# A two-block transformer on one core: first loads in smaller pieces, stacked compression operands, a scaling moved to GpSimd

## The reference, cut to what matters

```python
def first_block(x, ...):
    for l in range(2):
        x = x + 0.5 * swiglu(rms_norm(x, norm_ffn1[l]), w_ffn1_gate[l], w_ffn1_up[l], w_ffn1_down[l])
        x = x + hybrid_mixer(rms_norm(x, norm_mix[l]), w_in[l], ...)
        x = x + 0.5 * swiglu(rms_norm(x, norm_ffn2[l]), ...)
    return rms_norm(x, norm_final)

# inside the first block's mixer
def compress(k, pos, w1, w2):                 # 15 windows of 32 tokens, 2 kv heads: 30 rows
    blocks = k[:, :, cidx, :] + pos
    flat = blocks.reshape(B, G, n_cmp, CMP_LEN * Dh)      # 30 rows of 2048
    return jax.nn.gelu(flat @ w1) @ w2        # w1: 2048 x 256, w2: 256 x 64
kc = compress(k_cmp, pos_ck, w_ck1, w_ck2)
vc = compress(v_cmp, pos_cv, w_cv1, w_cv2)
...
return g[..., 0:1] * o_cmp + g[..., 1:2] * o_slc + g[..., 2:3] * o_win

def second_block(x, ...):                     # two layers: attention, then a SwiGLU FFN
    for l in range(2):
        x = hybrid_layer(...)
    return x                                  # the output
```

## Time and profile before

| | before |
|---|---|
| median of 3 runs | 1820.74 us |
| the profiled execution | 1821.47 us, span 1819.7 us |
| PE busy | 1789.9 us, 98% of the span |
| weight loads of PE busy | 1458.3 us, 80% |
| DVE / ACT / POOL busy | 1124.2 / 929.9 / 206.6 us |
| moved from memory | 173 GB/s over the span |

### The profile page before, as it was taken

How to read it: one execution, slowest core, us unless ns; L and a number is a source line. 1 busy time by engine, 2 the same in 40 slices (tenths; PEclk the granted TensorE clock), 3 DMA queues, 4 the chain that set the end, 5 groups by cost and what they waited for, 6 DMA issues and landing times.

```text
span 1819.7 us, 23649 instructions
## 1 busy us (share of the span) xinstructions
PE 1789.9 (98%) x8740; PEld 1458.3 (80%) x8740; DVE 1124.2 (62%) x1649; ACT 929.9 (51%) x1267; POOL 206.6 (11%) x226
## 2 busy tenths in 40 slices
PE   7999999999999999999999999999999999999999
PEld 6888887788888888877888877778888877788887
DVE  5555687655455555787555479966555589865553
ACT  6444475644444444565544276656444556644441
POOL 0000020000000000300000087200001393100000
PEclk9999999999999999999999999999999999999999
DMA  8556463455555554543554654445555554555551
GB/s 256 185 185 222 137 189 108 139 187 190 213 167 191 184 206 148 183 133 126 185 185 167 229 185 139 161 140 185 185 184 200 160 186 140 185 156 177 187 190 77
DMA packets 221017, 316.21 MB, mean 174 GB/s; under 512 B 14056, under 2 KB 162176, under 8 KB 220672
## 3 DMA queue, kind: packets, MB, share of 16 engines
q1 hardware_dynamic: 220928, 315.03, 53.0%
HBM read 313.94 MB, written 1.05 MB: 173 GB/s over the span
## 4 chain that ended last, share of the span: by engine, by line
PE 88%; DVE 7%; ACT 2%; DVEq 1%; issue 1%; DMA 1%; SPq 0%; ACTq 0%
PE ps L1843 27%; PE ps L1845 26%; PE ps L1844 26%; DVE w_lo L1157 2%; PE ps L1952 2%; PE ps L1853 1%; PE ps L2048 1%; ACT w_hi L679 1%; DVE score L1618 1%; PE ps L2036 1%; PE ps L1987 1%; PE ps L2024 1%; PE ps L2328 1%; DMA raw<-in_w_ffn_up 1%; DVEq L1621 0%
## 5 line engine op out<-in xcount | busy, mean ns | idle before, releaser
L1157 DVE TENSOR_TENSOR w_lo<-raw,w_hi 128x2048 fp32r<-128x2048 f32 (+1 forms) x297 | 675.1, 2297 | 233.0 <-ACT w_hi L679 232.1
L1843 PE MATMUL ps<-w_hi,aT_hi 128*128 128x512 f32 (+2 forms) x1728 | 688.9, 399 | 7.9 <-DVE w_lo L1310 4.8
L1845 PE MATMUL ps<-w_hi,aT_lo 128*128 128x512 f32 (+2 forms) x1728 | 670.4, 388 | 0.0
L1844 PE MATMUL ps<-w_lo,aT_hi 128*128 128x512 f32 (+2 forms) x1728 | 668.6, 387 | 0.0
L679 ACT ACTIVATE w_hi<-raw 128x2048 fp32r<-128x2048 f32 (+1 forms) x297 | 554.5, 1899 | 158.5 <-PE ps L1845 153.8
L1843 PEld LDWEIGHTS ps<-w_hi,aT_hi 128*128 128x128 f32 x1728 | 325.1, 188 | 84.8 <-issue 15.5
L1845 PEld LDWEIGHTS ps<-w_hi,aT_lo 128*128 128x128 f32 x1728 | 324.9, 188 | 68.2
L1844 PEld LDWEIGHTS ps<-w_lo,aT_hi 128*128 128x128 f32 x1728 | 325.7, 188 | 59.3
L729 ACT ACTIVATE att<-ps,rstd 128x256 f32<-128x256 f32 x132 | 55.5, 472 | 377.6 <-PE ps L1845 377.6
L1231 DVE SCALAR_TENSOR_TENSOR att<-ps,rstd,att 128x256 f32<-128x256 f32 x132 | 57.8, 479 | 287.2 <-ACT att L729 287.2
L1843 PE MATMUL ps<-w_hi,gT_hi 128*128 128x512 f32 x528 | 207.1, 392 | 0.0
(11 more groups left out here) (267 smaller groups left out, 1402.4 us busy)
## 6 DMA issues: line engine op xcount, KB each, us to landing
raw<-in_w_in SPq DMA_DIRECT2D x120, 512.0 KB, 4.5
raw<-in_w_ffn_gate SPq DMA_DIRECT2D x88, 512.0 KB, 4.2
raw<-in_w_ffn_up SPq DMA_DIRECT2D x88, 512.0 KB, 5.2
raw<-in_w_ffn_down SPq DMA_DIRECT2D x88, 512.0 KB, 4.4
raw<-in_w_ffn_in SPq DMA_DIRECT2D x88, 512.0 KB, 5.1
raw<-in_w_ffn_out SPq DMA_DIRECT2D x44, 512.0 KB, 4.7
raw<-in_w_out SPq DMA_DIRECT2D x32, 512.0 KB, 4.5
raw<-in_w_ck SPq DMA_DIRECT2D x8, 512.0 KB, 3.9
```

The costliest lines, as they stand in the source:

```text
L1157: V.tensor_tensor(o, a, h, ALU.subtract).then_inc(units_split, 1)
L1843: M(o, ah, wh, start=start, stop=False)
L1844: M(o, ah, wl, start=False, stop=False)
L1845: return M(o, al, wh, start=False, stop=stop)
```

## The change

Four things change.

1. **First loads.** `x` comes in four transfers of 128 rows by 512 columns, units 0 and 1 in halves (two transfers of 256 KB each), interleaved in the order of use; the gains are loaded from ACT's queue. Each quarter of `x` is turned by PE inside the first tile (`first_tile`), and the tile's order is (tokens 0, unit 0), (tokens 1, unit 0), (tokens 0, unit 1), (tokens 1, unit 1) in steps that wait for one quarter and one half unit each. PE does 8 and then 24 transposes of the identity, whose results nobody reads (`busy`). ACT's first table load comes ahead of the first data, and GpSimd makes `ident` before its other constants.
2. **Compression.** High and low parts of the windows lie side by side, 30 + 30 columns (`kflat`, `vflat`), so that one loaded operand holds both; with the high weights and the low weights that is four matmuls a step in place of six (the low-by-low product comes along). The 60 rows are copied out, and a product with `fold` (60x30, two identities on top of each other) turns and adds them; GELU comes after it, on the turned form.
3. **Scaling of the probabilities.** For pairs 0 to 6 of each layer (`SCALED1`) DVE multiplies reciprocal and gate (128x4), and GpSimd scales the probabilities in two TENSOR_TENSORs, 2x128 and 2x256 columns a partition. They stand ahead of `rotate(1304, 8)` in GpSimd's order. PE's `pair_turn(u)` in the compression stands one step later.
4. **The end.** The last 128 tokens are added and stored in two halves of 512 columns.

```diff
+SCALED1 = 7
...
-            def first_unit():
-
-                act.wait_ge(loaded[0], 32)
-                for h, signal in enumerate((half_hi, units_hi)):
-                    nc.scalar.activation(w_hi[:, 0, 1024 * h:1024 * h + 1024], raw[:, 0, 1024 * h:1024 * h + 1024], ACT.Copy)\
-                        .then_inc(signal, 1)
+            def first_half(j, h):
+
+                act.wait_ge(loaded[j] if h else half_loaded[j], 32)
+                part = slice(1024 * h, 1024 * h + 1024)
+                nc.scalar.activation(w_hi[:, j, part], raw[:, j, part], ACT.Copy).then_inc(units_hi if h else half_hi, 1)
...
+                for k in range(SCALED1):
+                    pool.wait_ge(pair_factors, l * SCALED1 + k + 1)
+                    for i, (c, n) in enumerate(((0, P), (P, 2 * P))):
+                        q = pair_p[:, k % 2, :, c:c + n]
+                        o = nc.gpsimd.tensor_tensor(q, q, lanes(pair_factor[:, k % 2, :, i], n), ALU.mult)
+                    o.then_inc(pair_scaled, 1)
                 projected(4)
                 rotate(1304, 8)
...
-                nc.scalar.activation(h1, ps[0:30, 1, :].rearrange("p (k n) -> p k n", k=2), ACT.Gelu_apprx_tanh)\
-                    .then_inc(gelu_done, 1)
+                nc.scalar.activation(h1, ps[0:60, 1, :].rearrange("p (k n) -> p k n", k=2), ACT.Copy)\
+                    .then_inc(h1_copied, 1)
                 exps(5)
                 probs_turned(4)
+                act.wait_ge(h1_T, l + 1)
+                nc.scalar.activation(h1T[:, :, :], ps[:, 6, 384:448].rearrange("p (k n) -> p k n", k=2)[:, :, 0:30],
+                                     ACT.Gelu_apprx_tanh)
+                nc.scalar.activation(vc_h1, ps[:, 6, 448:512].rearrange("p (k n) -> p k n", k=2)[:, :, 0:30],
+                                     ACT.Gelu_apprx_tanh).then_inc(gelu_done, 1)
...
+                        if i == 1 and last:
+                            if n == 0:
+                                dve.wait_ge(last_half, 1)
+                            else:
+                                o.then_inc(x_ready, 1)
+                                dve.wait_ge(units_used, st.used(p_last))
...
+                    if k < SCALED1:
+                        f = pair_factor[:, k % 2, :, :]
+                        assert gates[1] - gates[0] == 12
+                        V.tensor_tensor(f, f, gates1[:, :, gates[0]:gates[0] + 13:12].rearrange("p i e -> p e i"), ALU.mult)\
+                            .then_inc(pair_factors, 1)
+                        return
...
+            def first_turned(n):
+
+                pe.wait_ge(x_loaded[n], 16)
+                turned(x, *FIRST_PARTS[n])
+
+            def first_tile(st):
+
+                for n, (i, j) in enumerate(FIRST_PARTS):
+                    pe.wait_ge(stage_ready, n + 1)
+                    for c in range(4):
+                        if i == 0 and c == 0:
+                            pe.wait_ge(half_split, j + 1)
+                        if i == 0 and c == 2:
+                            split_ready(st, j)
...
+                        if (n, c) == (0, 0):
+                            first_turned(1)
+                        elif (n, c) == (0, 3):
+                            first_turned(2)
+                        elif (n, c) == (1, 3):
+                            first_turned(3)
...
+            def busy(n):
+
+                for _ in range(n):
+                    nc.tensor.transpose(ps[:, 3, 0:P], ident[:, :], ident[:, :])
+
+            pe.wait_ge(ident_ready, 1)
+            busy(8)
             pe.wait_ge(first_gains_loaded, 16)
             nc.tensor.transpose(ps[:, 0, 0:2 * KC], first_rows[:, :], ident[0:2 * KC, 0:2 * KC]).then_inc(gains_T, 1)
+            first_turned(0)
+            busy(24)
...
-                    if c == 2:
+                    if c == 3:
                         pair_turn(u)
...
-                            ah, al = h[:, 30 * k:30 * k + P], lo[:, 30 * k:30 * k + P]
-                            wh, wl = w_hi[:, st.slot(p), w:w + 256], w_lo[:, st.slot(p), w:w + 256]
+                            a = t[:, 60 * k:60 * k + P]
                             o = ps[:, 1, 256 * n:256 * n + 256]
-                            M(o, ah, wh, start=k == 0 and n == 0, stop=False, skip_group_check=True)
-                            M(o, ah, wl, start=False, stop=False, skip_group_check=True)
-                            o = M(o, al, wh, start=False, stop=k == 15, skip_group_check=True)
+                            M(o, a, w_hi[:, st.slot(p), w:w + 256], start=k == 0 and n == 0, stop=False, skip_group_check=True)
+                            o = M(o, a, w_lo[:, st.slot(p), w:w + 256], start=False, stop=k == 15, skip_group_check=True)
```

More of the change, by code:

```diff
@@ L227, in build @@
         rope_loaded = sem("rope_loaded")
-        x_loaded = [sem(f"x_loaded{i}") for i in range(2)]
+        x_loaded = [sem(f"x_loaded{k}") for k in range(4)]
+        half_loaded = [sem(f"half_loaded{j}") for j in range(2)]
+        ident_ready = sem("ident_ready")
+        last_half = sem("last_half")
         first_gains_loaded = sem("first_gains_loaded")
@@ L1304, in other_gains, with first_half @@
                 rope()
[L1306 to L1314 removed]
+            def first_half(j, h):
+                dve.wait_ge(units_hi if h else half_hi, j + 1)
+                part = slice(1024 * h, 1024 * h + 1024)
+                V.tensor_tensor(w_lo[:, j, part], raw[:, j, part], w_hi[:, j, part].bitcast(F32), ALU.subtract)\
+                    .then_inc(units_split if h else half_split, 1)
             dve.wait_ge(gains_T, 1)
@@ L1929, in wide_pair @@
                                           w_lo[:, st.slot(p + d), w:w + 512], False, d == 1 and c == 1)
+                                if late is None and (i, d, n, c) == (1, 1, 0, 1):
+                                    o.then_inc(last_half, 1)
                         if i == 1:
@@ L2028, in pair_turn @@
                 def pair_turn(k):
-                    pe.wait_ge(pair_probs, J + (k + 1))
+                    if k < SCALED1:
+                        pe.wait_ge(pair_scaled, l * SCALED1 + k + 1)
+                    else:
+                        pe.wait_ge(pair_probs, l * (PAIRS1 - SCALED1) + k - SCALED1 + 1)
                     if k > 0:
```

173 lines of the change are left out of this document (103 added, 70 removed).

## The result

The changed kernel took 1806.31 us, the median of four runs (1806.16 to 1807.21), beside 1820.62 (1820.34 to 1821.35) for the kernel before in the same job: a ratio of 0.992, with a 95% interval of 0.9908 to 0.9933. That is 14.3 us; 13.7 were forecast.

What follows compares the result with a forecast made beforehand. PE, busy 98% of the span, was taken as the bound, except at the start, where it waits for loads and splits. Start -5.4, compression -7.5 and end -0.8 sum to -13.7: 1807.0 us from 1820.74, range 1803.5 to 1812.5.

Steps and rivals of the forecast that it cites:

- First product at 10.0, second tile at 22.2: Start: products run at 0.227 us from 10.0 behind the 24 transposes; second tile at 22.2 instead of 27.74, worth -5.4 us.
- The dummies raise PE's level: Start: the identity transposes whose results nobody reads bring PE to its faster level; otherwise the start gains only 2.5 us.
- The first rival: Start: PE's level stays low under transposes, so the start gains only 2.5 us, 1809.9 us in all; chance 0.22.
- The compression, -3.35 and -4.15: First and second layer: 32 products fewer (-3.8 each) and old waits gone (1.1, 1.9), less 1.55 of new waits.
- The lock doesn't bite, thanks to the gap of 1.57 us: Compression: copy and `masked` before DVE's next split let GpSimd's scaling start first; the split waits some 0.15 us.
- the second rival: Compression: DVE's splits lock GpSimd out, or pairs otherwise set the pace; about +2.5 us a layer, 1812 us; chance 0.16.
- a late turn isn't paid again in each round: Compression: the next pairs' scores are issued a whole unit ahead, so one late `pair_turn` does not delay each later round.
- the slower rival: Compression's `pair_turn`s: GpSimd takes 5.5 us a pair instead of 1.65; if all showed, 1838 us; chance 0.03.
- Folding costs nothing: Compression: four folding products replace four transposes of the same size, so PE's time changes by nothing.
- The end, -0.8 (0.6 to 1.2): Kernel's end: last store starts 0.6 us earlier, and half the bytes may save up to 0.6 in landing.
- the fourth rival: Same as the slower rival: GpSimd at 5.5 us a pair delays the `pair_turn`s, up to 1838 us; chance 0.03.
- The rival that everything is early: Start and compression: products from about 9 us, no waits for pairs; -17.4 or half that excess, 1803 to 1805; chance 0.1.

## Why the prediction was right

The forecast was -13.7, the runs gave -14.3 (-15.2 and -14.9 in the two later jobs). The compression and the end were right in mechanism, the start in all but one step: start -5.7 for -5.4, compression -8.0 for -7.5, end -1.2 for -0.8, and 0.6 us given back between them, for which the forecast had nothing. Point by point:

- **First product at 10.0, second tile at 22.2.** Measured 9.46 and 22.08 in this profile, 8.60 to 8.79 and 21.2 to 21.4 in others. The step that failed is "PE does not start there, since 24 transposes of the identity stand ahead": they began at 4.71, not 5.5, and ended at 8.1 here and at 7.6 in another profile, since the level rose early among them. What PE waited for was half 0a's remainder, which came at about 9.3 here and at 8.5 in the other two, where 8.8 was forecast. Only in the profile with the first product at 8.79 did the transposes stand ahead, until some 0.3 us after the half was ready. The term is -5.7 here and -6.4 and -6.5 in the other profiles, for -5.4; that it fits so well in the profile shown is in part luck, since this execution's half came late.
- **The dummies raise PE's level.** Shown: without them the products stay 0.43 us apart until 13.54, and it costs 2.0 us. The first rival is out. The rule of the Trainium skill that transposes don't engage the full clock ("TensorE: Matmul & The Clock Gate", Part 4: PE-mode transpose) is not borne out: behind these transposes alone the products are 0.23 us apart.
- **The compression, -3.35 and -4.15.** Measured -3.77 and -4.21. ACT's round was 4.36 (4.5 forecast) and did become the slowest; DVE's split waited for ACT, not for GpSimd. The mis-sized terms are the waits at the first two turns: 0.2 and 0.8 us where the working had 0.5 and 1.05.
- **The lock doesn't bite, thanks to the gap of 1.57 us.** That the lock is there, and that the gap lets GpSimd start first, is shown by taking the gap away: operations of 2.59 us at pairs 2 and 3. The gap alone would not quite do, since GpSimd needs 0.25 + 1.61 us; the rest is DVE's wait for ACT, by 0.04 us at the closest. The 18.5 us of that run are not the price of the second rival (2.5 us a layer in the working), since the factor was moved as well; that price stays unmeasured. The run also shows that "a late turn isn't paid again in each round", the argument against the slower rival, hangs on the order: with the factor behind the masked operations it was paid again, 18.5 us over six late pairs, more than the 13.7 of the forecast. For the changed kernel's own order no run tests it.
- **Folding costs nothing.** Wrong by about half a microsecond a layer. It takes eight instructions, 1.07 us in the profile after, where four transposes stood before. From the product ahead to the product behind it is 1.32 us in place of 0.84 (267.44 to 268.76, 276.93 to 277.77):
```profile
277.44 0.40 PE L2136 MATMUL ps<-ident,tt 30*128 30x30 f32 x4
```
These 0.5 us are in the +0.26 and +0.23 behind the two compressions. In the second layer the wait of 0.4 us for GELU, which is gone, makes up for part of them; in the first, 0.2 us ahead of the folding do, and I don't know their cause.
- **The end, -0.8 (0.6 to 1.2).** Measured -1.18 in the profiles. The mis-sized term is the landing, of whose 0.6 us I took a third; all of it came.
- **No regression of the sort that the fourth rival names,** and no wait over 2 us in the tiles with pairs 4 to 6. The rival that everything is early (1803 to 1805) came half true: the start did reach -6.5 in one profile, but PE still waited in the compression.

The parts of the compression that I priced one behind the other don't add: the expectation for DVE's scaling (3.4 us) came from the same working as the forecast and was short by 2.6, because a pace that is 0.6 us a pair too slow is paid at every turn and the first one besides (2.40 us).

## What to carry to other kernels

An elementwise operation moved to GpSimd was cheap here only while a gap without a subtraction of two SBUF operands on VectorE followed its release: find the gap in the timeline, compare its length with the operation's, and keep it. When products are taken away from a full TensorE, look for the slowest round of the engines that feed it and shorten that in the same change, since stacking alone gave much less than its count of instructions. A late operand costs its wait, and sometimes the time at TensorE's lower level behind it as well: waits of 2.06, 1.91 and 2.88 us were followed by it, waits of 2.40 and 2.66 were not.

## What the runs showed of the hardware

- A float32 product of 60x30 was issued as two instructions and took 0.27 us; a transpose of 30x30 was one and took about 0.1 (0.40 for four).
- GpSimd and a DVE split held each other up in more than one place, in both directions: scaling 2.59 us in place of 0.61, split 3.17 and 4.45 in place of 2.29. At one place of the second block the loser changed from one trace to another. The runs of the two kernels whose traces have the long split lie up to 1.6 and 2.3 us apart, and the traced one is at the top each time; that the split is the cause is not shown.
- A wait of PE of 2 to 3 us is not always followed by its lower level. With the late factor, five of six were, and the one of 2.66 us was not. Where DVE scales the pairs, the products behind 2.40 us at 250.00 are 0.12 us apart; behind 2.30 us at 1050.72 they are 0.43 apart, seven of them. What decides it no run here shows.
- Transposes of 128x128 in float32 raised PE's level. In this start the granted clock in the windows reads 1.00 while products are 0.43 us apart (without dummies, 10 to 12 us); with the late factor it reads 0.73 over the 10 us that hold the doubled spacing. At the very start the spacing tells the level and the granted clock doesn't:
```profile
10.00:12.00 2.00, 2.00 (x8) 1.69 (x7) 0.00 (x0) 0.78 (x4) 0.00 (x0) 1.00 1.08 372
```
- The first product moves by 0.9 us between executions (8.60 to 9.46), and the second tile moves with it (21.20 to 22.08). The 24 transposes took from 2.86 to 4.45 us in nine profiles with the same start. A change to a start wants more than one profile.
